# The mixer stage of a hybrid decoder layer rebuilt: loads, scan loop and the second mixer's front in another order

## What is computed

```python
h = concat([meta_tokens, x])                       # 272 tokens
proj = rmsnorm(h, norm1_gain) @ w_in               # 1024 -> 4608
u, q, fpre, v, og, gates = split(proj)             # 512 x 5, then 2 x 1024
# S5: 32 groups of 64 complex states, s_t = lam_bar * s_{t-1} + b_bar @ u_t
y = gelu(real(c @ s) + d_skip * u);  y_s5 = y * sigmoid(y @ w_glu)
# HGRN2: f = lb + (1 - lb) * sigmoid(fpre); logf = log(f); k = 1 - f; q = silu(q)
# S_t = diag(f_t) S_{t-1} + k_t v_t^T;  o_t = S_t^T q_t
y_hg = rmsnorm_heads(o) * gn_gain * silu(og)
h = h + (sigmoid(g1) * (y_s5 @ w_branch_s5) + sigmoid(g2) * (y_hg @ w_branch_hgrn)) @ w_out
h = h + moe(rmsnorm(h, norm2_gain))                # top 4 of 32 experts, clamped SwiGLU
return rmsnorm(h, final_norm_gain)[:, 16:]
```

## Time and profile before

| | |
|---|---|
| device time, median of 3 runs | 1265.72 us (1265.67 to 1266.29) |
| the profiled execution | 1266.21 us, span 1264.4 us |
| TensorE busy | 1210.8 us (96%) |
| VectorE, ScalarE, GpSimd busy | 469.7, 153.0, 42.4 us |
| mean granted TensorE clock | 0.977 of full speed |
| moved from memory | 434.53 MB, 344 GB/s over the span |

### The profile page before, as it was taken

One profiled execution on the slowest core, in us unless ns is written; L12 is line 12 of the kernel. 1 busy time (PEld: TensorE's weight loads), 2 busy tenths in 40 slices (PEclk: granted clock), 3 DMA queues, 4 the chain that ended last, 5 costly groups with the idle time before them and its releaser, 6 DMA issues.

```text
span 1264.4 us, 14304 instructions
## 1 busy us (share of the span) xinstructions
PE 1210.8 (96%) x5529; PEld 518.1 (41%) x5529; DVE 469.7 (37%) x1034; ACT 153.0 (12%) x286; POOL 42.4 (3%) x53
## 2 busy tenths in 40 slices
PE   6989899999899999999999999999999999999996
PEld 6664578984433333333333333333333333333332
DVE  4899966332322332222232322222232322222224
ACT  1232241221100000000000000000000000000001
POOL 0134300000000000000000000000000000000000
PEclk7999898999899999999999999999999999999999
DMA  7213331093699999999999999999999999999993
GB/s 204 100 67 133 134 132 69 11 425 86 279 427 428 427 429 429 428 429 429 428 429 429 427 429 429 428 429 429 428 429 429 428 429 429 428 429 429 427 429 157
DMA packets 47281, 435.92 MB, mean 345 GB/s; under 512 B 9924, under 2 KB 9992, under 8 KB 22616
## 3 DMA queue, kind: packets, MB, share of 16 engines
q1 hardware_dynamic: 41832, 434.49, 82.1%
q10 hardware_dynamic: 5424, 1.10, 0.5%
HBM read 434.53 MB, written 1.05 MB: 344 GB/s over the span
## 4 chain that ended last, share of the span: by engine, by line
PE 72%; DMA 13%; DVE 5%; issue 1%; ACT 0%; POOL 0%; POOLq 0%; SPq 0%; DVEq 0%; ACTq 0%
PE ps L558 68%; DMA ring<-in_w_gate_up 13%; PE ps L561 4%; DVE ring L930 2%; DVE ring L936 0%; DVE ring L1073 0%; DVE ring L933 0%; DVE ring L1119 0%; DVE w_mix L936 0%; DVE rout L933 0%; DVE w_mix L1388 0%; DVE x L930 0%; ACT ring L390 0%; DVE rout L936 0%; DVE w_mix L1226 0%
## 5 line engine op out<-in xcount | busy, mean ns | idle before, releaser
L558 PE MATMUL ps<-ring,w_mix 128*64 128x512 f32 (+1 forms) x3168 | 720.0, 602 | 9.6 <-DMA ring<-in_w_gate_up 7.8
L558 PEld LDWEIGHTS ps<-ring,w_mix 128*64 128x64 f32 (+1 forms) x3168 | 228.3, 137 | 477.4 <-issue 448.0
L933 DVE TENSOR_SCALAR w_mix<-ps 128x512 f32<-128x512 f32 x64 | 41.3, 687 | 608.9 <-PE ps L558 608.9
L558 PE MATMUL ps<-ring 128*128 128x256 f32 (+6 forms) x928 | 226.6, 408 | 15.3 <-POOL ring L375 11.3
L558 PEld LDWEIGHTS ps<-ring 128*128 128x128 f32 (+2 forms) x928 | 158.7, 192 | 80.2 <-issue 37.7
L558 PE MATMUL ps<-w_mix 64*128 64x512 f32 (+3 forms) x624 | 143.7, 573 | 1.1 <-ACT w_mix L390 1.1
L390 ACT ACTIVATE w_mix<-ps 128x512 f32<-128x512 f32 (+1 forms) x104 | 51.4, 527 | 389.5 <-PE ps L558 339.4
L930 DVE TENSOR_TENSOR ring<-ring 128x256 f32<-128x256 f32 (+5 forms) x140 | 82.8, 623 | 22.2 <-PE ps L558 12.8
L930 DVE TENSOR_TENSOR x<-ps,x 128x512 f32<-128x512 f32 x136 | 84.4, 682 | 16.1 <-PE ps L558 16.1
L558 PEld LDWEIGHTS ps<-w_mix 64*128 64x128 f32 (+3 forms) x624 | 51.9, 162 | 89.9 <-issue 86.8
L390 ACT ACTIVATE w_mix<-w_mix 128x512 f32<-128x512 f32 x32 | 20.1, 629 | 520.4 <-DVE w_mix L933 520.4
(11 more groups left out here) (134 smaller groups left out, 287.4 us busy)
## 6 DMA issues: line engine op xcount, KB each, us to landing
ring<-in_w_gate_up SPq DMA_DIRECT2D x128, 2048.0 KB, 24.8
ring<-in_w_down SPq DMA_DIRECT2D x64, 2048.0 KB, 27.6
ring<-in_w_in SPq DMA_DIRECT2D x9, 2048.0 KB, 7.9
ring<-in_w_out SPq DMA_DIRECT2D x1, 4096.0 KB, 13.3
w_mix<-in_w_branch_s SPq DMA_DIRECT2D x1, 2048.0 KB, 12.5
w_mix<-in_w_branch_hgrn SPq DMA_DIRECT2D x1, 2048.0 KB, 13.3
x<-in_x SPq DMA_DIRECT2D x2, 512.0 KB, 5.8
w_mix<-in_s_w_glu SPq DMA_DIRECT2D x1, 1024.0 KB, 10.1
```

The source lines that it names most:

```text
L558: return nc.tensor.matmul(o, l, r, start=start, stop=stop, skip_group_check=True)
L933: return V.tensor_scalar(o, i, s1, s2, op0, op1) if op1 is not None else V.tensor_scalar(o, i, s1, None, op0)
```

## The change

It has five parts. (1) GpSimd loads the meta tokens and the small rows, SP the B and C matrices behind the first group of `w_in`; on ScalarE the constants come last. (2) In the head VectorE forms the first S5 rows before it normalises x, in the waits between; ScalarE takes the first exponents before the roots, and scales and copies the C matrices. (3) In the loop VectorE does both parts of the back rotation; GpSimd does nothing. The large number is added on ScalarE. `bu` is done for two tiles at a time, `y_of` for four, for which `xre` and `xim` have eight buffers instead of two, and there are three projection tiles per pair of tiles (`LOOP_TILES`) instead of two. (4) ScalarE does the affine part of f, k = 1 - f and the two sigmoids of q and og straight after the loop, and the logarithm before GELU. VectorE takes the cumulative sums first, then the S5 output, q and GELU, and the level operations among the rest; `dec` has two buffers, and differences are made one or two levels ahead. (5) TensorE's order after the loop: three projection tiles, the diagonal product, the turn of `kh`, level 0, a tile, half of the GLU product, level 1, the other half, level 2, a tile, level 3, a tile, the state products, level 4, a tile, level 5, a tile, level 6. All four gate sigmoids stand ahead of the `o_mm` wait on ScalarE. Buffers move in the ring; `C_GC` has two more columns with the sign for C.

The core of the diff (SP, GpSimd, ScalarE, TensorE, VectorE):

```diff
+        LOOP_TILES = [(2, 1), (2, 1), (2, 1), (1, 2), (2, 1), (2, 1), (2, 1), (2, 1)]
...
                 sp.dma_start(x[:, t, :], x_d[:, t, :]).then_inc(s["xload%d" % t], 16)
-            sp.dma_start(xm[:, :], a["meta_tokens"]).then_inc(s["meta"], 16)
-            pr = lambda n, k: a[n].rearrange("l (k p) -> (l k) p", p=P)
-            sp.dma_start(prow[0:8, :], pr("norm1_gain", 8)).then_inc(s["rows"], 16)
-            sp.dma_start(prow[8:16, :], pr("norm2_gain", 8)).then_inc(s["rows"], 16)
-            sp.dma_start(prow[16:24, :], pr("hgrn_lb_logits", 8)).then_inc(s["rows"], 16)
-            sp.dma_start(prow[24:28, :], pr("hgrn_norm_gain", 4)).then_inc(s["rows"], 16)
-            sp.dma_start(grow[:, :], a["norm2_gain"].rearrange("l (i c) -> (l i) c", c=2 * P)).then_inc(s["grow_in"], 16)
...
                 g = GROUPS[n]
                 sp.dma_start(win[n % 2], win_d[:, :, g * 512:(g + 1) * 512]).then_inc(s["win%d" % (n % 2)], 16)
+                if n == 0:
+                    sp.dma_start(bre, a["s5_b_re"].rearrange("l (i g) p h -> (g p) (l i) h", g=2)).then_inc(s["bload"], 16)
+                    sp.dma_start(bim, a["s5_b_im"].rearrange("l (i g) p h -> (g p) (l i) h", g=2)).then_inc(s["bload"], 16)
+                    sp.dma_start(cn[:, 0], a["s5_c_re"].rearrange("l (t g) h p -> (g h) (l t) p", t=4)).then_inc(s["cload"], 16)
+                    sp.dma_start(cn[:, 1], a["s5_c_im"].rearrange("l (t g) h p -> (g h) (l t) p", t=4)).then_inc(s["cload"], 16)
                 if n == 2:
...
-            z = slice(META, TOK)
-            for i in range(ST):
-                pool.wait_ge(s["scanned"], i + 1)
-                if i >= 1:
-                    pool.wait_ge(s["xim5"], i)
-                if i >= 2:
-                    pool.wait_ge(s["ysum"], i - 1)
-                nc.gpsimd.tensor_tensor(out=pool_rot[0][:, z], in0=zre[:, z], in1=sinT[i % 2][:, z], op=ALU.mult)
-                nc.gpsimd.tensor_tensor(out=pool_rot[1][:, z], in0=zim[:, z], in1=cosT[i % 2][:, z], op=ALU.mult)\
-                    .then_inc(s["pool_turned"], 1)
-                pool.wait_ge(s["pool_turned"], i + 1)
-                nc.gpsimd.tensor_tensor(out=xim[i % 2][:, z], in0=pool_rot[0][:, z], in1=pool_rot[1][:, z], op=ALU.add)\
-                    .then_inc(s["xim5"], 1)
+            pr = lambda n, k: a[n].rearrange("l (k p) -> (l k) p", p=P)
+            pool.dma_start(prow[0:8, :], pr("norm1_gain", 8)).then_inc(s["rows"], 16)
+            pool.dma_start(xm[:, :], a["meta_tokens"]).then_inc(s["meta"], 16)
+            pool.dma_start(prow[8:16, :], pr("norm2_gain", 8)).then_inc(s["rows"], 16)
+            pool.dma_start(prow[16:24, :], pr("hgrn_lb_logits", 8)).then_inc(s["rows"], 16)
+            pool.dma_start(prow[24:28, :], pr("hgrn_norm_gain", 4)).then_inc(s["rows"], 16)
+            pool.dma_start(grow[:, :], a["norm2_gain"].rearrange("l (i c) -> (l i) c", c=2 * P)).then_inc(s["grow_in"], 16)
+            pool.dma_start(prow[28:32, :], a["s5_d"].rearrange("l (k g) h -> (l k) (g h)", k=4)).then_inc(s["rows"], 16)
...
-            act.dma_start(cst[:, :], a["shape_consts"]).then_inc(s["consts"], 16)
             act.dma_start(s5r[:, 0, :], a["s5_lambda_re"].rearrange("l (i g) p -> (l i) (g p)", g=2)).then_inc(s["s5rows"], 16)
             act.dma_start(s5r[:, 1, :], a["s5_lambda_im"].rearrange("l (i g) p -> (l i) (g p)", g=2)).then_inc(s["s5rows"], 16)
             act.dma_start(small[0:ST, 0:2], a["s5_log_dt"].rearrange("l (i g) -> (l i) g", g=2)).then_inc(s["s5rows"], 16)
-            act.dma_start(bre, a["s5_b_re"].rearrange("l (i g) p h -> (g p) (l i) h", g=2)).then_inc(s["bload"], 16)
-            act.dma_start(bim, a["s5_b_im"].rearrange("l (i g) p h -> (g p) (l i) h", g=2)).then_inc(s["bload"], 16)
-            act.dma_start(cn[:, 0], a["s5_c_re"].rearrange("l (t g) h p -> (g h) (l t) p", t=4)).then_inc(s["cload"], 16)
-            act.dma_start(cn[:, 1], a["s5_c_im"].rearrange("l (t g) h p -> (g h) (l t) p", t=4)).then_inc(s["cload"], 16)
+            act.dma_start(cst[:, :], a["shape_consts"]).then_inc(s["consts"], 16)
...
-                if i >= 1:
-                    act.wait_ge(s["rounded"], i)
-                f(turns, steps, ACT.Identity, scale=s5c[:, 1, i:i + 1]).then_inc(s["ph"], 1)
+
+                if i >= 2:
+                    act.wait_ge(s["rounded"], i - 1)
+                link(f(turns[i % 2], steps, ACT.Identity, scale=s5c[:, 1, i:i + 1]))
+                f(rnd[i % 2], turns[i % 2], ACT.Identity, bias=zero_c[:, 3:4]).then_inc(s["ph"], 1)
...
             for i in range(ST):
+                before, after = LOOP_TILES[i // 2]
+                if i % 2 == 0:
+                    next_proj(LOOP_TILES[i // 2 - 1][1] if i >= 2 else 0)
+                else:
+                    next_proj()
                 if i + 1 < ST:
                     sines_of(i + 1)
                 if i + 2 < ST:
                     turns_of(i + 2)
-                next_proj()
-
+                if i == 0:
+                    act.wait_ge(s["c_turned"], 1)
+                    for c in range(2):
+                        last = f(blk[:, 2 + c, :, :], ps[6 + c][:, :].rearrange("p (a n) -> p a n", a=4), ACT.Copy)
+                    last.then_inc(s["c_laid"], 1)
+                if i % 2 == 1:
+                    next_proj(before - 1)
+
+            act.wait_ge(s["acol"], 1)
+            link(f(small[:, 20:24], small[:, 16:20], ACT.Sigmoid, scale=-1.0))
+            f(small[:, 24:28], small[:, 20:24], ACT.Identity, scale=-1.0, bias=ones[:, 0:1])
+            link(f(kT, kT, ACT.Sigmoid))
+            for h in range(HEADS):
+                last = f(kT[:, h, :], kT[:, h, :], ACT.Identity, scale=small[:, 24 + h:25 + h], bias=small[:, 20 + h:21 + h])
+            link(last)
+            f(sg, qT, ACT.Sigmoid).then_inc(s["q_sig"], 1)
+            f(osg, ogT[:, :, :], ACT.Sigmoid).then_inc(s["og_sig"], 1)
+            next_proj(LOOP_TILES[-1][1])
+            f(bT, kT, ACT.Ln).then_inc(s["logf"], 1)
+            f(kc.rearrange("p (a n) -> p a n", a=KW), kT[:, :, META:TOK], ACT.Identity, scale=-1.0, bias=ones[:, 0:1])
+            act.wait_ge(s["logf"], 1)
+            f(kT[:, :, 0:META], kT[:, :, 0:META], ACT.Identity, scale=-1.0, bias=ones[:, 0:1]).then_inc(s["kc_ready"], 1)
...
-            def bu(i):
-
-                if i >= 2:
-                    pe.wait_ge(s["bu_free"], i - 1)
-                r = 32 * (i % 4)
+            def bu(p):
+
+                if p >= 1:
+                    pe.wait_ge(s["bu_free"], 2 * p)
                 for c in range(2):
-                    last = mm(ps[2 + 2 * (i % 2) + c][:, 0:TOK], blk[r:r + 32, c, i // 4, :], uT[r:r + 32, i // 4, :], True, True)
+                    for j in range(2):
+                        i = 2 * p + j
+                        r = 32 * (i % 4)
+                        last = mm(ps[2 + 2 * j + c][:, 0:TOK], blk[r:r + 32, c, i // 4, :], uT[r:r + 32, i // 4, :], True, True)
                 last.then_inc(s["bu"], 1)
 
-            def y_of(i):
-
-                pe.wait_ge(s["xs5"], i + 1)
-                pe.wait_ge(s["xim5"], i + 1)
-                r, t = 32 * (i % 4), i // 4
-                o = ps[6 + t // 2][r:r + 32, (t % 2) * SEQ:(t % 2 + 1) * SEQ]
-                mm(o, blk[:, 2, t, r:r + 32], xre[i % 2][:, META:TOK], True, False)
-                mm(o, blk[:, 3, t, r:r + 32], xim[i % 2][:, META:TOK], False, True).then_inc(s["ysum"], 1)
+            def y_of(t):
+
+                pe.wait_ge(s["xs5"], 4 * t + 4)
+                if t == 0:
+                    pe.wait_ge(s["c_laid"], 1)
+                for c in range(2):
+                    for j in range(4):
+                        r = 32 * j
+                        o = ps[6 + t // 2][r:r + 32, (t % 2) * SEQ:(t % 2 + 1) * SEQ]
+                        last = mm(o, blk[:, 2 + c, t, r:r + 32], (xre, xim)[c][(4 * t + j) % 8], c == 0, c == 1)
+                last.then_inc(s["ysum"], 1)
...
+            for p in range(ST // 2):
+                project(LOOP_TILES[p][0])
+                if p >= 2 and p % 2 == 0:
+                    y_of(p // 2 - 1)
+                if 2 * p + 2 < ST:
+                    bu(p + 1)
+                project(LOOP_TILES[p][1])
+            y_of(ST // 4 - 1)
...
             for i in range(ST):
                 re, im = ps[2 + 2 * (i % 2)][:, 0:TOK], ps[3 + 2 * (i % 2)][:, 0:TOK]
                 sn, co = sinT[i % 2], cosT[i % 2]
+                dve.wait_ge(s["bu"], i // 2 + 1)
+                dve.wait_ge(s["sines"], i + 1)
                 if i >= 1:
                     dve.wait_ge(s["xs5"], i)
-                dve.wait_ge(s["bu"], i + 1)
-                dve.wait_ge(s["sines"], i + 1)
                 tt(rot[0], re, co, MU)
-                tt(rot[1], im, sn, MU)
+                n01 = mark(tt(rot[1], im, sn, MU))
                 tt(rot[2], im, co, MU)
-                link(tt(rot[3], re, sn, MU))
-                tt(rot[0], rot[0], rot[1], AD).then_inc(s["bu_free"], 1)
```

(33 more changed lines are left out.)

438 lines of the change are left out of this document (223 added, 215 removed).

## The result

| | before | after |
|---|---|---|
| median of the runs, us | 1265.74 (4 runs) | 1226.80 (4 runs, 1223.31 to 1227.16) |
| ratio to before | | 0.9695, 95% interval 0.9683 to 0.9706 |
| profiled execution: time, span, us | 1266.2, 1264.4 | 1226.91, 1225.1 |
| mean granted clock | 0.977 | 0.981 |

The account below looks back on a forecast made before the run. VectorE was taken to bound the loop and TensorE to pace most of what follows up to `o_mm`. Head -11.5, loop and after -35.1, handoffs +3 gave -43.6 from 1266.2, stated as 1222.5 us, range 1212 to 1241.

Parts of the forecast that it names:

- first exponent waits only for landing: Head: ScalarE issues four short loads, so its first exponent waits only for data to land; VectorE's list runs from 5.8.
- bound of 3.8 us per load on GpSimd: Head: at 3.8 us for each of seven small loads, the last is issued at 27 and the head's gain is gone.
- rival 1: Head: loads on GpSimd or SP eat the gain, which falls to 2 us; kernel 1232 us; chance 0.12.
- my lower bound: Loop: VectorE's SBUF products without GpSimd take 0.38 us each, with bounds 0.35 and 0.72.
- VectorE stays the bound, with almost no slack: Loop: TensorE's work per pair of iterations takes 11.8 to 12.5 us beside VectorE's 12.6, so VectorE remains the bound.
- rival 2: Loop: TensorE becomes the bound through non-overlapping row groups and drains of some 0.3; pair 13.6 us, kernel 1232; chance 0.13.
- 1.5 us for ScalarE's late phase at the value tiles: Loop: at the two 512-column value tiles ScalarE's next phase comes after a late copy, +1.5 us.
- the handoffs: Whole sum: some thirty signal waits of about 0.1 us, which the hand schedule leaves out, add 3 us.
- The logarithm: After the loop: ScalarE's chain ends 4.9 us after the loop; VectorE and everything behind in its order wait for it.
- 5.3 us before the loop ends: After the loop: when ScalarE, having copied the last but one tile, starts its chain to the logarithm.
- The copies: After the loop: copies and small operations take 1.3 us of ScalarE's chain to the logarithm.
- The clock: After the loop: TensorE idles some 3 us before the diagonal product, then runs at the 1.2 GHz level, +2.5 us.

Follow-up runs that it names:

- e2: Changed kernel with the four B and C loads issued by ScalarE again; 1241.14 us, ratio 0.9813.
- e11: Changed kernel with GpSimd's seven small loads back on SP, behind x and ahead of the weights; 1222.56 us, ratio 0.9665.
- e10: Changed kernel with the rounding of the phase moved from ScalarE back to VectorE; 1224.55 us, ratio 0.9673.
- e1: Changed kernel with the imaginary half of the back rotation given back to GpSimd; 1223.71 us, ratio 0.9675.
- e7: Changed kernel with two projection tiles beside each pair of iterations instead of three, the eight others behind the loop; 1240.84 us, ratio 0.9827.
- e3: Changed kernel with ScalarE's two gate copies moved ahead of its wait for the kh differences; 1220.39 us, ratio 0.9654.
- e4: Changed kernel with ScalarE's chain to the logarithm put between its copies in the last two loop iterations; 1218.04 us, ratio 0.9625.
- e12_states_split: e9_head_order with the states' four 16-row products moved ahead of a projection tile, apart from the four of 128 rows; 1209.58 us, ratio 0.9560.
- e9_head_order: e8 with VectorE's head reordered: x variances earlier, angle reduction behind the products for xnT; 1210.79 us, ratio 0.9564.
- e5: Changed kernel with TensorE's last projection tile moved from ahead of the seventh level's products to behind them; 1223.08 us, ratio 0.9673.
- e6: Changed kernel with a pair's four bu products in scan-tile order instead of alternating row groups; 1226.38 us, ratio 0.9695.
- e8: Changed kernel with the moves of e4 and e5, the last sines ahead of a copy, and log_dt loaded first; 1212.30 us, ratio 0.9585.

## Why the prediction was right

**What bounds the kernel: right.** The expert stage is unchanged at 933 us, and 39.8 us at `o_mm` are 39.6 at the first expert and 39.3 in the span.

**The head: right in its mechanism, 1.5 us too good.** Forecast -11.5, measured -10.0. That ScalarE's "first exponent waits only for landing" was right, but the landing ends at 7.6 and not before VectorE's first x at 5.8; this costs 2.2 us; VectorE's list behind it took 12.0, not 12.4 (`xnT` ready at 19.96). e2 shows the B and C loads as the cause. The bound of 3.8 us per load on GpSimd, and rival 1 with it, was far off: the seven issues took 0.52 to 0.65 us each, and e11 shows nothing lost or won by them. I had called these loads 2 to 4 KB; one of them, the meta tokens, is 64 KB, and its issue took 0.52 us too.

**The loop: right in VectorE's durations, wrong in who bounds it.** Forecast 101.5, measured 97.2. The products came at 0.35, my lower bound, not 0.38, and the groups lost the gaps between them, so that an iteration is 5.69 us, not 6.3 (the four products from PSUM to the sums behind them: 1.40 us from start to start, 1.52 in the earlier trace rows). The step that failed is "VectorE stays the bound, with almost no slack": at 5.69 two iterations (11.4 us) are shorter than TensorE's part of a pair, three tiles, `bu` and half a `y_of` (12.1 us; the loop's 97.17 us are eight of them). This is rival 2's mechanism without its price. Its price needed drains and no overlap; `bu` took 1.19 us against the 1.0 forecast, and at a change of tile shape (near 60, 71, 72 and 73 us) the next product starts 0.31 to 0.32 us behind the last, against 0.22 to 0.23 within a shape: 0.1 us and not 0.3. e10, e1 and e7 say the same from three sides: 1.4 and 4.7 us more of loop on VectorE leave TensorE standing 8.6 and 9.2 us (8.6 in the changed kernel), fewer tiles do shorten the loop, and then cost more behind it. The 1.5 us for ScalarE's late phase at the value tiles were 6.1, but VectorE waited there while TensorE worked.

**Behind the loop: 71.1 forecast with the handoffs, 78.0 measured.** Three terms. The logarithm: 9.5 instead of 4.9, because "5.3 us before the loop ends" for ScalarE's copy became 0.7, with VectorE quicker and TensorE not; the chain itself took 10.1 us as forecast. The copies: I priced them as ScalarE's time, 1.3 us, and did not ask who waits for them. The two gate copies stand behind `kh`'s exponent, which waits for VectorE, which waits for the logarithm, and TensorE has two banks: 5.19 us. The clock: I gave one fall 2.5 us; three came, two of them at waits, and a trace with fewer (e11) has TensorE busy for 5.2 us less.
The first two are one term and not two: with the copies moved and the logarithm late (e3) TensorE stands 1.1 us less, with the logarithm early and the copies where they were (e4) 5.2 us less.

**Sum.** -10.0, -13.2 in the loop, -16.5 behind it: -39.7 against -43.6. The errors in the loop (4.3 too slow) and behind it (6.9 too quick) belong together: by TensorE's tiles the logarithm was ready at 145.6, by the forecast at 143.9, however early VectorE left the loop. The total is nearer than its terms for that reason and not because they were right: the mechanism of the loop was wrong, and its error of 4.3 us took back half of the 8.4 in the other two.

**Table loads.** The load at 135.89 begins as the copy ahead of it ends (135.49 and 0.39), takes 1.28 us, and the operation behind it begins at 137.18; it is the same in the earlier trace rows. The drain of 1.38 us that the Trainium skill (ScalarE: Activation LUTs, What ACT_TABLE_LOAD costs) puts on each switch shows in neither trace.

## What to carry to other kernels

When work is moved beside a loop until "almost no slack" is left, do the sum for both engines with the *lower* bounds of each: whichever is the bound decides what the next idle wait will be, and a price on the other engine then costs little (e1, e10). For every copy out of PSUM, name the engine that waits for the bank and what stands ahead of the copy on its own engine; then look for what waits next, because moving the copy alone may only uncover it (e3), and moving the late result frees both (e4). Where the clock moves by itself, split a stretch with the same work into busy and standing time before an experiment is called a gain. The best kernels found, e12_states_split and e9_head_order, which the runs do not tell apart, are 4.4% faster than before and some 1.4% faster than the change, by nothing but order: ScalarE's chain to the logarithm beside the last iterations, its last sines ahead of a late copy, one tile kept for the last wait, and VectorE's head in order of what TensorE needs.

## What was new in the hardware

TensorE's clock fell without any idle time of TensorE: in the traces of the changed kernel, e2, e4, e5, e6, e8, e9 and e10, eight in all, beside or just behind the 16-row and 128-row products in turn, not in those of e1, e3, e7 and e11, which have the same products, and not in e12, where they are apart. Runs of one kernel differ with their clock by 3 to 5 us (e4: 1215.0 and 1215.9 us at 0.989 and 0.990, 1220.2 and 1220.6 at 0.986). What decides it in one run and not another is open, and so is whether these products bring it.

A single issue of these B and C loads held its engine for 10.30 us on SP, and for 6.73 and 9.73 us on ScalarE (e2): the block goes with the loads, whoever issues them. Which of the four loads blocks is not the same (one of B on SP, one of B and one of C on ScalarE); why is not shown.

Four small products in two row groups took 1.19 us in either order (e6), the time of two alone in the kernel before (four instructions at 295 ns, 1.18 us).
